# Transposing three of four tiles of attention probabilities by 32x32 blocks and a DMA exchange, with the loads at the end of the branch reordered

## What is computed

```python
S = 1024; MLA_HEADS = 8; MLA_NOPE = 128; MLA_ROPE = 64; MLA_V = 128
def attend(qblk):                       # 128 queries of every head
    s = jnp.einsum('bhqd,bhkd->bhqk', qblk, k_t).astype(jnp.float32) * scale
    p = jax.nn.softmax(s, axis=-1)      # over 1024 keys
    return jnp.einsum('bhqk,bhkd->bhqd', p.astype(v_t.dtype), v_t)
```

## Time and profile before

| | |
|---|---|
| median of 3 runs | 1961.65 us (1957.78 to 1962.82) |
| the profiled execution | 1961.58 us, span 1959.3 us |
| mean granted clock of TensorE | 0.983 |
| TensorE busy | 1869.9 us, 95% of the span |
| VectorE, ScalarE busy | 1373.2 us (70%), 1066.3 us (54%) |
| attention by steps | about 128 to 561 us |

### The profile page before, as it was taken

One profiled execution on the slowest core, in us unless ns is written; L12 is line 12 of the kernel. 1 busy time (PEld: TensorE's weight loads), 2 busy tenths in 40 slices (PEclk: granted clock), 3 DMA queues, 4 the chain that ended last, 5 costly groups with the idle time before them and its releaser, 6 DMA issues.

```text
span 1959.3 us, 26754 instructions
## 1 busy us (share of the span) xinstructions
PE 1869.9 (95%) x9179; PEld 1574.2 (80%) x9179; DVE 1373.2 (70%) x1829; ACT 1066.3 (54%) x1737; POOL 135.3 (7%) x147
## 2 busy tenths in 40 slices
PE   8989999999489999999999999997799999999997
PEld 8978888887368888888888888886688888888886
DVE  5477777777355657565765437835799898998986
ACT  6576666665244334242534222423677777877775
POOL 1021111010000000000000000000000101101010
PEclk9999999999789999999999999998899999999999
DMA  6125454554621111111454544343999999999993
GB/s 207 44 63 129 105 116 107 112 119 108 161 71 44 55 44 47 40 58 29 151 164 137 172 154 161 126 194 118 371 390 401 391 402 400 391 398 390 400 391 78
DMA packets 180666, 364.30 MB, mean 186 GB/s; under 512 B 29377, under 2 KB 99905, under 8 KB 180417
## 3 DMA queue, kind: packets, MB, share of 16 engines
q1 hardware_dynamic: 174784, 346.33, 51.6%
q0 software_dynamic: 4752, 16.78, 3.4%
q10 hardware_dynamic: 1040, 0.00, 0.0%
HBM read 308.37 MB, written 54.69 MB: 185 GB/s over the span
## 4 chain that ended last, share of the span: by engine, by line
PE 84%; DVE 6%; DMA 5%; ACT 2%; issue 1%; SPq 1%; POOL 1%; DVEq 0%; ACTq 0%; POOLq 0%
PE ps L1195 23%; PE ps L1197 23%; PE ps L1196 23%; PE ps L1184 5%; PE ps L1282 3%; PE ps L1491 1%; DMA probs_T<-squares_T 1%; PE ps L1503 1%; DMA carry<-rows_T 1%; PE ps L1321 1%; PE ps L1320 1%; DVE row_max L2042 1%; PE ps L1475 1%; PE ps L1501 1%; SPq L836 1%
## 5 line engine op out<-in xcount | busy, mean ns | idle before, releaser
L1807 DVE TENSOR_TENSOR w_lo<-w_raw,w_hi 128x1024 fp32r<-128x1024 f32 x384 | 442.6, 1218 | 54.8 <-ACT w_hi L3287 54.7
L3287 ACT ACTIVATE w_hi<-w_raw 128x1024 fp32r<-128x1024 f32 x384 | 371.0, 1053 | 0.5 <-PE ps L1197 0.4
L1195 PE MATMUL ps<-w_hi,xeT_hi 128*128 128x512 f32 x512 | 201.2, 393 | 1.0 <-DVE w_lo L1807 0.9
L1197 PE MATMUL ps<-w_hi,xeT_lo 128*128 128x512 f32 x512 | 199.8, 390 | 0.0
L1196 PE MATMUL ps<-w_lo,xeT_hi 128*128 128x512 f32 x512 | 199.2, 389 | 0.0
L1807 DVE TENSOR_TENSOR d_lo<-d_raw,d_hi 128x1024 fp32r<-128x1024 f32 (+1 forms) x66 | 67.2, 1027 | 143.2 <-ACT d_hi L2925 138.5
L1195 PE MATMUL ps<-hT_parts,d_hi 128*128 128x512 f32 x368 | 145.5, 395 | 0.0
L1197 PE MATMUL ps<-hT_parts,d_lo 128*128 128x512 f32 x368 | 144.1, 392 | 0.0
L1196 PE MATMUL ps<-hT_parts,d_hi 128*128 128x512 f32 x368 | 144.1, 392 | 0.0
L1102 POOL TENSOR_TENSOR stat<-stat,minus_half 128x4 f32<-128x4 f32 (+3 forms) x56 | 54.3, 970 | 1165.2 <-DVE stat L1804 1165.1
L2925 ACT ACTIVATE d_hi<-d_raw 128x1024 fp32r<-128x1024 f32 x42 | 44.5, 1060 | 157.1 <-PE ps L1197 87.7
(11 more groups left out here) (454 smaller groups left out, 4304.8 us busy)
## 6 DMA issues: line engine op xcount, KB each, us to landing
w_raw<-in_w_gate_e SPq DMA_DIRECT2D x128, 512.0 KB, 6.9
w_raw<-in_w_up_e SPq DMA_DIRECT2D x128, 512.0 KB, 7.0
w_raw<-in_w_down_e SPq DMA_DIRECT2D x128, 512.0 KB, 5.8
d_raw<-in_w_in SPq DMA_DIRECT2D x80, 256.0 KB, 3.3
probs_T<-squares_T SPq DMA_DIRECT2D x124, 128.0 KB
pT_lo<-probs_T SPq DMA_DIRECT2D x31, 512.0 KB, 3.4
gates_T<-stage SPq DMA_DIRECT2D x16, 512.0 KB, 2.9
sg<-gates_T SPq DMA_DIRECT2D x16, 512.0 KB, 3.5
```

The lines of the kernel that those rows point to most:

```text
L1195: pe.matmul(out_ap, a_hi, b_hi, start=start, stop=False)
L1197: return pe.matmul(out_ap, a_lo, b_hi, start=False, stop=stop)
L1807: return dve.tensor_tensor(dst, whole, high.bitcast(F32), ALU.subtract)
L3287: nc.scalar.activation(w_hi[:, n % RING, :], w_raw[:, n % RAW, :], ACT.Copy).then_inc(hi_ok, 1)
```

## The change

`by_dma` now takes tiles 0, 1 and 2 of every four, up to tile 56: 43 tiles, where it took 31. The tiles of the last head after its first go by TensorE. `dma_count(t)` counts the tiles by DMA up to t, and takes the place of t // 2 in the waits. VectorE's blocks are made of every fourth key (`c b j` for `c j b`), so that one write of 128 rows of 4 KB lays the tile into HBM, and the read gathers four pieces of 1 KB for each partition. At the end of the branch one transfer of 4 MB in step (7, 2) takes the place of the eight of `load_rows`, and the first weights are issued in step (7, 4) for (7, 6). ScalarE's `rows_high` waits for the one transfer.

```diff
--- before.py
+++ after.py
@@ -157,7 +157,7 @@
 
 
 def by_dma(t):
-    return 0 <= t < 8 * MH - 2 and t % 2 == 0
+    return 0 <= t <= 8 * (MH - 1) and t % 4 != 3
 
 
 def by_tensor(t):
@@ -166,6 +166,10 @@
 
 def tensor_count(t):
     return sum(by_tensor(u) for u in range(t + 1))
+
+
+def dma_count(t):
+    return sum(by_dma(u) for u in range(t + 1))
 
 
 def parts_count(t):
@@ -234,7 +238,7 @@
     h2_dram = nc.dram_tensor("h2_rows", (S, D), F32, kind="Internal").ap()
 
     h_dram = nc.dram_tensor("rows_T", (KD, P, S), F32, kind="Internal").ap()
-    p_dram = nc.dram_tensor("probs_T", (SLOTS, P, Q4, NT * SQ), F32, kind="Internal").ap()
+    p_dram = nc.dram_tensor("probs_T", (SLOTS, Q4, P, NT * SQ), F32, kind="Internal").ap()
     inv_dram = nc.dram_tensor("inverse_sums", (2, HALF), F32, kind="Internal").ap()
     oa_dram = nc.dram_tensor("gla_out_T", (KD, P, S), F32, kind="Internal").ap()
     ob_dram = nc.dram_tensor("mla_out_T", (KD, P, S), F32, kind="Internal").ap()
@@ -637,7 +641,7 @@
         p1_ok = Later(lat_sq, NT)
         u_ok = Later(lat_ev, NT)
         s_sig = Later(latT_act, 7)
-        g_out = [Later(h_out, 32), Later(hT_in, 16 * KD)]
+        g_out = [Later(h_out, 32), Later(hT_in, 16)]
         rows_out = Later(inv_out, 32 * MH)
         ffn_in = Later(inv_in, 32 * MH)
         f_mm = Later(s_mm, NT * MH)
@@ -829,19 +833,17 @@
                 sp.dma_start(ob_dram[h, :, cols], obS[:]).then_inc(ob_out, 16)
 
             def turn_probs(t):
-                d, group = t // 2, t // Q4
+                d, group = dma_count(t) - 1, t // Q4
                 sp.wait_ge(sq_ok, d + 1)
-                rows = p_dram[d % SLOTS].rearrange("(j b) q x -> b j q x", b=SQ)
-                for q in range(Q4):
-                    sp.dma_start(rows[:, :, q, :],
-                                 squares_T[q * SQ:(q + 1) * SQ].rearrange("b j c a -> b j (c a)")).then_inc(p_out, 16)
-                sp.wait_ge(p_out, 16 * Q4 * (d + 1))
+                sp.dma_start(p_dram[d % SLOTS].rearrange("q (b j) x -> (q b) (j x)", j=Q4),
+                             squares_T[:].rearrange("p j c a -> p (j c a)")).then_inc(p_out, 16)
+                sp.wait_ge(p_out, 16 * (d + 1))
                 if d:
                     sp.wait_ge(p_in, 16 * d)
                 if group >= 2:
                     sp.wait_ge(pv_mm, group - 1)
-                sp.dma_start(probs_part(pT_lo, t).bitcast(F32),
-                             p_dram[d % SLOTS].rearrange("p q (c a) -> p q c a", a=SQ)).then_inc(p_in, 16)
+                sp.dma_start(probs_part(pT_lo, t).bitcast(F32).rearrange("p q c a -> p q (c a)"),
+                             p_dram[d % SLOTS].rearrange("q p x -> p q x")).then_inc(p_in, 16)
 
             def store_inverse(h, half):
                 m = 2 * h + half
@@ -856,15 +858,9 @@
                 sp.wait_ge(inv_out, 16 * m + 16)
                 if m and m < 2 * MH - 1:
                     sp.wait_ge(ob_out, 16 * m)
+                if m == 2 * MH - 1:
+                    sp.wait_ge(p_out, 16 * dma_count(NT * MH - 1))
                 sp.dma_start(inverse_at(h, half), spread(inv_dram[half], HALF)).then_inc(inv_in, 16)
-
-            def load_rows(k):
-                if k == 0:
-                    sp.wait_ge(h_out, 32)
-                    sp.wait_ge(seam_tr, MH * 8)
-                else:
-                    sp.wait_ge(hT_in, 16 * k)
-                sp.dma_start(hT_again[:, k, :], h_dram[k]).then_inc(hT_in, 16)
 
             load_ukv(2)
             for i, n in STEPS:
@@ -882,6 +878,10 @@
                     store_ob(i - 1, 0)
                     if i < MH:
                         spread_inverse(i - 1, 1)
+                    if i == MH - 1:
+                        sp.wait_ge(h_out, 32)
+                        sp.wait_ge(seam_tr, MH * 8)
+                        sp.dma_start(hT_again, h_dram.rearrange("k p s -> p k s")).then_inc(hT_in, 16)
                 if n == 4:
                     if i + 2 < MH:
                         load_uq(i + 2)
@@ -891,15 +891,11 @@
                         store_inverse(i, 0)
                     if 0 < i < MH:
                         store_ob(i - 1, 1)
+                    if i == MH - 1:
+                        load_gla(0, 0)
+                        load_gla(0, 1)
                 if n == 6:
                     spread_inverse(i, 0)
-                if n == 6 and i == MH - 1:
-                    load_gla(0, 0)
-                    load_gla(0, 1)
-                if n % 2 == 0 and 8 * (MH - 1) + 2 <= 8 * i + n:
-                    for k in range(2):
-                        if 8 * i + n - 8 * (MH - 1) - 2 + k < KD:
-                            load_rows(8 * i + n - 8 * (MH - 1) - 2 + k)
             store_ob(MH - 1, 1)
 
 
@@ -2053,8 +2049,8 @@
             def probs_squares(t):
                 dve.wait_ge(exp_ok, t + 1)
                 if t:
-                    dve.wait_ge(p_out, 16 * Q4 * (t // 2))
-                dve.transpose(squares_T[:], probs[:, t % 2, :].rearrange("p (c j b) -> p j c b", c=NT, j=Q4)) \
+                    dve.wait_ge(p_out, 16 * (dma_count(t) - 1))
+                dve.transpose(squares_T[:], probs[:, t % 2, :].rearrange("p (c b j) -> p j c b", c=NT, j=Q4)) \
                     .then_inc(sq_ok, 1)
 
             def probs_low(t):
@@ -2901,14 +2897,14 @@
                                          ACT.Copy).then_inc(pt_hi, 1)
 
             def turned_high(t):
-                act.wait_ge(p_in, 16 * (t // 2) + 16)
+                act.wait_ge(p_in, 16 * dma_count(t))
                 nc.scalar.activation(probs_part(pT_hi, t), probs_part(pT_lo, t).bitcast(F32), ACT.Copy).then_inc(pt_hi, 1)
 
             def exponentials(i, n):
                 t = 8 * i + n
                 act.wait_ge(max_ok, t + 1)
                 if by_dma(t - 2):
-                    act.wait_ge(sq_ok, (t - 2) // 2 + 1)
+                    act.wait_ge(sq_ok, dma_count(t - 2))
                 elif t >= 2:
                     act.wait_ge(p_tr, 2 * tensor_count(t - 2))
                 if i and n % Q4 == 0:
@@ -2955,7 +2951,7 @@
                 take(1, g)
 
             def rows_high(k):
-                act.wait_ge(hT_in, 16 * (k + 1))
+                act.wait_ge(hT_in, 16)
                 nc.scalar.activation(hT_hi[:, k, :], hT_again[:, k, :], ACT.Copy,
                                      scale=g_mix_c[:, k:k + 1]).then_inc(hT_hi_ok, 1)
```

## The result

The changed kernel takes 2029.58 us (2028.38 to 2030.93, 4 runs) beside 1961.61 for the kernel before (4 runs): ratio 1.035, 95% interval 1.0332 to 1.0368. That is 68 us slower. I had said slower, 1977, within 1946 to 2003. The sign and the place were right, the size was not.

What follows compares the result with a forecast made beforehand. TensorE was taken to bound heads 0 to 6, and SyncE's in-order transfers head 7. 1961.6 + 32 for the new waits - 18 for the end = 1975.6, one more for head 0: 1977 us, range 1946 to 2003.

Steps and rivals of the forecast that it cites:

- What bounds it: TensorE without a gap in heads 0 to 6; in head 7, waits on transfers that SyncE issues in order.
- Tiles moved: Heads 0 to 6: tiles 1 and 5 leave TensorE, 11.1 us could be gained; VectorE's 2.2 us a head hidden.
- The new wait: Steps 2 and 6: VectorE's blocks wait for the previous tile's write; 5.0 us lost a head, from 1.5 to 7.4.
- rival E: Strided blocks cost double: 1.24 us more in steps 2 and 6 of seven heads, 17 us: 1994; chance 0.09.
- rival D: TensorE's clock also drops after idling in step 6: 1.6 us more a head, 1988, top 2005; chance 0.12.
- The order of keys: VectorE's blocks read every fourth element; taken at 1.24 us each, upper bound twice that.
- The exchange: One write for four and a read in 1 KB pieces; write near 2.9 us, read taken at no cost.
- The end of the branch: Head 7: first weights about 43 us into it, 17 us gained, plus 1 in the tail: 18 us, 11 to 25.
- B: Single write lands early, heads lose 1.5 us or less, end gains most: 1952, down to 1945; chance 0.20.
- F: TensorE's 11 us gained in full and the end too: 1933, needing writes 7 us after the inverse store; chance 0.05.
- C: Heads' loss and the end's gain cancel: a head loses about 2.9 us, 1956 to 1967; chance 0.14.
- A: The forecast itself: steps 6 and 2 wait for the writes; 1977, within 1968 to 2000; chance 0.40.

Runs made afterwards that it cites:

- e9: Changed kernel with inverse sums stored as 128 pieces of 16 bytes (other order) and VectorE's blocks read without stride; 1929.0 us, ratio 0.984.
- e8: e4 with the inverse sums stored as 128 pieces of 16 bytes, in another order; 1925.9 us, ratio 0.981.
- e3: Changed kernel with inverse sums stored as 128 pieces of 16 bytes instead of 512 of 4, in another order; 1945.4 us, ratio 0.989.
- e14: e4 with inverse sums turned by one more VectorE transposition and stored as 16 pieces of 128 bytes, right order; 1923.0 us, ratio 0.981.
- e1: Changed kernel with VectorE's blocks made of 32 neighbouring keys again (no stride); 2037.0 us, ratio 1.035.
- e5: Changed kernel with only every other tile by DMA, so tiles 1 and 5 are on TensorE again; 1947.4 us, ratio 0.992.
- e13: Changed kernel with inverse sums turned by one more VectorE transposition and stored as 16 pieces of 128 bytes, right order; 1940.2 us, ratio 0.989.
- e4: Kernel before with only the new end of the branch; even tiles, four writes and old key order stay; 1948.6 us, ratio 0.991.
- e6: Changed kernel with the store of the inverse sums issued behind the exchange of tile 0 or 4, not ahead; 2038.4 us, ratio 1.040.
- e15: e4 with the store of the inverse sums issued behind tile 0's and tile 4's exchange, as in e6; 1939.2 us, ratio 0.989.
- e10: Changed kernel with the store of the inverse sums issued by ScalarE on its own queue, in steps 1 and 5; 2069.5 us, ratio 1.052.
- e12: e4 with the store of the inverse sums, pieces of 4 bytes, issued by ScalarE on its own queue; 1989.0 us, ratio 1.011.

## Why the prediction was right and wrong

*What bounds it* was right: TensorE without a gap, 0.6 us to spare ahead of the seam's projection, and a write that the inverse sums hold up. *Where it shows* was right too: VectorE's blocks of steps 2 and 6, with row maximum, seam and projection behind.

*Tiles moved.* TensorE's own work in a head did fall, to 64.9 - 11.0 - 4.1 = 49.8 us, from 51.2 (51.7 with 0.5 idle). But the 11 us of seven heads were not to be had even with hardly a late write: e9 takes 51.1 us a head, 0.4 less than e8, and e3 1.0 more. "Hidden as a sum, though perhaps not where it lands" should have had a price. VectorE's chain in a step is the second limit, as TensorE's waits in e3, e9 and e14 suggest.

*The new wait* is the term that was mis-sized: 5.0 us a head forecast, 13.2 measured. It breaks into three.
- I took 5.0 between 1.5 and 7.4, leaving room for writes landing 8.2 us after the inverse sums. None did: 11.1 to 12.1 in all twelve, as the earlier trace rows had it for the tiles' own writes. The early landing of the earlier trace rows was that of a store of the outputs, and I had no reason to prefer it to the tiles' rows. The top, 7.4, was the value that the tiles' own rows gave. That is 2.4 us.
- The blocks behind the wait take 0.77 us more, twice a head, 1.5 us. I had the stride as rival E with a condition that held (2.01 us, 1.6 times 1.24), but valued it apart from the wait.
- The clock, rival D: 4.1 us a head for the 1.6 that I gave it ((1 - 0.52) x 2 us twice is 1.9, so that was off by itself), mostly because it fell in both steps (3.3 and 6.4 us idle) and not in step 6 alone: 1.6 us of it is step 2's, for which I had nothing, and 2.5 step 6's.

7.4 + 1.5 + 4.1 = 13.0 for 13.2. The three terms were all in the prediction, as a bound and two rivals, and I treated as alternatives what adds up: a longer wait is what makes the clock fall. That split is bookkeeping from the trace, and its parts are not independent: by e1 the 1.5 us does not come back when the stride goes, for the wait then grows. Added up in this way, in hindsight, the sum of the prediction is 1961.6 + 7 x 13.0 - 2.6 - 18 + 1 = 2033, 3 us from the result.

*The order of keys.* The Trainium skill's rule (SBUF — State Buffer, Door 1: The DMA port swizzle), that each access to a new line of 16 bytes pays, agrees with the traces: the blocks take 2.01 us when every fourth element is read, and 1.24 in order (e1). I kept the low value against it. In the changed kernel it makes no difference (e1), in one without late writes 10 to 16 us (e3 against e9).

*The exchange* costs nothing, as said (e5). A write with nothing small near it is counted 2.6 to 2.9 us after its issue (e13, the changed kernel).

*The end of the branch:* 18 us gained forecast, 16.2 measured here and 18 alone (e4). The sum came out partly by luck. The load of 4 MB took 20.5 us for 13 to 17, and the weights came 49.5 us into head 7 (559.09 to 608.61) for 43, beyond my outer bound of 48, with the store of the inverse sums between them in the queue. So ahead of the weights only 11.7 us were gained for 17; the 4.5 us behind them, where I had 1, made up for most of it: the next weights, for which ScalarE had waited 4.80 us, are no longer late. e13 shows what the pieces cost there: with larger ones the load takes 14.8 us, and the weights come 26.8 us behind head 6's last sums for 41.0.

*Rivals.* B, F and C needed early writes and fell. A held in kind and happened with D and E on top of it. The Trainium skill's rule about the count, weighed in the prediction at 8.0 us behind the inverse sums, gave too little: the trace's 11 to 12 us is what decided.

## What to carry to other kernels

When the profile shows one transfer made of many tiny pieces, look at what every other write near it takes, and remove it first: here a change that looked 3.5% bad was 1% good without it, and a layout in which VectorE waits only 8.3 us for such writes had 20 us in it (e4 to e8). What was left of good came from the new end (e4: 0.9%); the moved tiles themselves were worth nothing or less, since e13 stands 0.9% above e14. Moving such a store behind something moved the bill to the next write (e6) or, where there was room, gave back a part (e15), and with another queue the bill was larger (e10, e12). Cutting it into larger pieces removed it, for 0.2 us of VectorE each time. And rivals that share a cause (a stall, the slower clock after it, a longer instruction behind it) are terms of one sum, so the upper end of the range is their total.

## What the runs showed of the hardware

- A store of 512 pieces of 4 bytes (2 KB in all) to HBM lands 8.0 us after its issue when nothing stands behind it (kernel before). In the changed kernel a 512 KB write issued 2 to 4 us behind it, on the same queue, is counted 7.1 to 9.3 us after its own issue, in twelve places, for 2.6 to 2.9 us where it is read off with nothing small near it. On another queue one was counted 9.6 us after its issue (e10). With 128 pieces of 16 bytes such a write takes 2.6 to 3.8 us (e3), with 16 of 128 bytes 2.6 to 3.1 (e13).
- The load of 4 MB next to such a store landed 20.5 us after its issue, and 14.8 us with 16 pieces of 128 bytes (changed kernel, e13).
- A 32x32 block transposition of 128x1024 fp32 on VectorE takes 2.01 us when it reads every fourth element (changed kernel) and 1.24 us when it reads them in order (e1).
- TensorE's granted clock fell to its lower level, 0.50, with the idle stretches of 3.3 and 6.4 us in head 3 of the changed kernel, and stayed there for 3 to 5 us of the work behind them.
